# Latent attention: the even block's exponential behind the last step's high part, the odd block's maximum in two parts, the extra turns in the last step

## The reference, cut to what matters

```
def _attend_dense(q, k, v):
    s = einsum('bqhd,bkhd->bhqk', q, k) * (QK_DIM ** -0.5)
    pr = softmax(s, axis=-1)
    return einsum('bhqk,bkhd->bqhd', pr, v)
...
k_all = concatenate([k_lat, k_ctx], axis=1)      # 1024 latent + 256 context keys
v_all = concatenate([v_lat, v_ctx], axis=1)
o = lax.map(lambda qi: _attend_dense(qi, k_all, v_all), qb)   # blocks of 128 queries
...
return (ga * (attn_o @ w_o_attn) + gb * (four_o @ w_fourier)) @ w_out
```

## Time and profile before

| | |
|---|---|
| median of three runs | 2403.45 us |
| the profiled execution's own time | 2400.3 us |
| its span | 2398.5 us |
| PE busy over the span | 94% |
| DVE, ACT busy over the span | 60%, 43% |
| granted TensorE clock, mean | 0.974 |
| attention's units, first maximum to last exponential | 1536 to 1859 us |

### The profile page before, as it was taken

One profiled execution on the slowest core, in us unless ns is written; L12 is line 12 of the kernel. 1 busy time (PEld: TensorE's weight loads), 2 busy tenths in 40 slices (PEclk: granted clock), 3 DMA queues, 4 the chain that ended last, 5 costly groups with the idle time before them and its releaser, 6 DMA issues.

```text
span 2398.5 us, 27813 instructions
## 1 busy us (share of the span) xinstructions
PE 2244.9 (94%) x11294; PEld 1861.8 (78%) x11294; DVE 1434.9 (60%) x2191; ACT 1023.1 (43%) x1586; POOL 273.4 (11%) x362
## 2 busy tenths in 40 slices
PE   5999899999999999999999998898898999499997
PEld 4898787888888888878888787677777775378886
DVE  6667535454554454467422138767667645689997
ACT  4677424122122122144321135466666313378785
POOL 2011001010010011000000015400000100111121
PEclk9999999999999999999999999999999999699998
DMA  3122611232332342232222021000000621989996
GB/s 141 45 71 80 224 49 53 75 119 96 110 129 91 97 145 95 90 116 41 75 88 68 25 73 46 18 1 1 1 1 30 235 75 52 352 317 378 388 387 203
DMA packets 79184, 280.71 MB, mean 117 GB/s; under 512 B 9872, under 2 KB 10000, under 8 KB 77392
## 3 DMA queue, kind: packets, MB, share of 16 engines
q1 hardware_dynamic: 48240, 172.77, 20.0%
q0 software_dynamic: 29664, 101.96, 13.6%
q10 hardware_dynamic: 1152, 4.19, 0.4%
HBM read 243.24 MB, written 35.66 MB: 116 GB/s over the span
## 4 chain that ended last, share of the span: by engine, by line
PE 77%; DVE 13%; ACT 7%; DMA 2%; issue 1%; POOLq 0%; SPq 0%; ACTq 0%; DVEq 0%
PE psum L98 23%; PE psum L99 23%; PE psum L100 23%; DVE small L2603 3%; ACT PB L2537 3%; DVE MP_lo L2640 2%; ACT MP_hi L2567 1%; PE psum L1015 1%; PE psum L2472 1%; PE psum L988 1%; DVE w_lo L232 1%; DMA gal<-gas 1%; PE psum L2483 1%; PE psum L3212 1%; PE psum L2985 1%
## 5 line engine op out<-in xcount | busy, mean ns | idle before, releaser
L98 PE MATMUL psum<-U_hi,w_hi 128*128 128x512 f32 (+1 forms) x1216 | 480.5, 395 | 14.5 <-DVE w_lo L232 9.3
L99 PE MATMUL psum<-U_lo,w_hi 128*128 128x512 f32 (+1 forms) x1216 | 477.9, 393 | 0.0
L100 PE MATMUL psum<-U_hi,w_lo 128*128 128x512 f32 (+1 forms) x1216 | 476.9, 392 | 0.0
L223 ACT ACTIVATE w_hi<-raw 128x1024 fp32r<-128x1024 f32 (+2 forms) x163 | 162.4, 1002 | 305.4 <-PE psum L100 300.8
L98 PEld LDWEIGHTS psum<-U_hi,w_hi 128*128 128x128 f32 (+1 forms) x1216 | 229.3, 189 | 68.7 <-issue 10.7
L100 PEld LDWEIGHTS psum<-U_hi,w_lo 128*128 128x128 f32 (+1 forms) x1216 | 229.3, 189 | 50.5 <-issue 0.8
L99 PEld LDWEIGHTS psum<-U_lo,w_hi 128*128 128x128 f32 (+1 forms) x1216 | 229.6, 189 | 47.4 <-issue 0.5
L232 DVE TENSOR_TENSOR w_lo<-raw,w_hi 128x1024 fp32r<-128x1024 f32 (+2 forms) x163 | 188.8, 1166 | 109.6 <-ACT w_hi L223 109.2
L98 PE MATMUL psum<-a_hi,w_hi 128*128 128x512 f32 x512 | 199.2, 389 | 0.0
L99 PE MATMUL psum<-a_lo,w_hi 128*128 128x512 f32 x512 | 199.2, 389 | 0.0
L100 PE MATMUL psum<-a_hi,w_lo 128*128 128x512 f32 x512 | 199.2, 389 | 0.0
(11 more groups left out here) (407 smaller groups left out, 4689.6 us busy)
## 6 DMA issues: line engine op xcount, KB each, us to landing
rawe<-in_w_e SPq DMA_DIRECT2D x112, 512.0 KB, 15.2
mraw<-in_w_mod POOLq DMA_DIRECT2D x128, 256.0 KB, 2.9
rawx<-in_w_e SPq DMA_DIRECT2D x56, 512.0 KB, 16.3
raw<-in_w_up SPq DMA_DIRECT2D x32, 512.0 KB, 3.6
raw<-in_w_dn SPq DMA_DIRECT2D x32, 512.0 KB, 3.6
raw<-in_w_e SPq DMA_DIRECT2D x24, 512.0 KB, 16.0
X<-in_xT SPq DMA_DIRECT2D x4, 1024.0 KB, 9.4
raw<-in_w_q SPq DMA_DIRECT2D x8, 512.0 KB, 4.4
```

The lines of the kernel that those rows point to most:

```text
L98: e.matmul(o, l[0], r[0], start=first, stop=False, skip_group_check=skip)
L99: e.matmul(o, l[0], r[1], start=False, stop=False, skip_group_check=skip)
L100: return e.matmul(o, l[1], r[0], start=False, stop=last, skip_group_check=skip)
L223: act.e.activation(w_hl[x.place][0][:, 0:x.width], w_raw[x.slot][:, 0:x.width], ACT.Copy).then_inc(w_hi, 1)
```

## The change

Four things change, all in the order of work or in what waits for what; no matmul, no transfer and no tile is added or taken away.

1. The exponential of the even block goes from step t = 3 to t = 4, and so behind the high part of step 4 on ACT. It waits for `part(m + 1, 0)`, not for its own maximum alone.
2. The maximum of the odd block is taken in two parts: columns 0 to 255 (the half bank it shares with the even block) right behind the even block's maximum at t = 2, columns 256 to 1279 at t = 4, and then the smaller of the two negated results (`larger`). The wait of the odd block's maximum for the even block's exponential is gone.
3. The extra turns: `turn_q` part 1 goes from (g, t) = (3, 1) to (3, 4), `turn_k` part 1 from (1, 1) to (1, 4), and parts 0 and 2 of `turn_k` change places, so that the one at (0, 1) is the small one.
4. In the merge, the last iteration no longer prepares the tile behind `T_AO[6] + 4`; its high and low part are made one place later.

```
     nmx = small[:, 0:8]
+    nmp = [small[:, 24 + 2 * i:26 + 2 * i] for i in range(2)]
...
-        x = {(2, 4): ("turn_q", h + 2, 0), (3, 1): ("turn_q", h + 2, 1), (0, 1): ("turn_k", h + 1, 0),
-             (0, 4): ("turn_k", h + 1, 2), (1, 1): ("turn_k", h + 1, 1)}.get((g, t))
+        x = {(2, 4): ("turn_q", h + 2, 0), (3, 4): ("turn_q", h + 2, 1), (0, 1): ("turn_k", h + 1, 2),
+             (0, 4): ("turn_k", h + 1, 0), (1, 4): ("turn_k", h + 1, 1)}.get((g, t))
...
-        m = {0: 2 * u + 3, 3: 2 * u + 4}.get(t, -1)
+        m = {0: 2 * u + 3, 4: 2 * u + 4}.get(t, -1)
...
         def exponential(m):
-            act.wait_ge(*at_s.dve("max", m))
+            act.wait_ge(*(at_s.dve("max", m) if m % 2 else at_s.dve("part", m + 1, 0)))
...
         def largest(m):
             dve.wait_ge(*at_s.pe("logits", m))
-            if m % 2:
-                dve.wait_ge(*at_s.act("exp", m - 1))
             dve.e.tensor_reduce(nmx[:, m % 8:m % 8 + 1], s_of(m), AX.X, ALU.max, negate=True).then_inc(
                 *at_s.dve.one("max", m))
+
+        def part(m, i):
+            dve.wait_ge(*at_s.pe("logits", m - 1 + i))
+            dve.e.tensor_reduce(nmp[m // 2 % 2][:, i:i + 1], s_of(m, *((256, TA) if i else (0, 256))), AX.X, ALU.max,
+                                negate=True).then_inc(*at_s.dve.one("part", m, i))
+
+        def larger(m):
+            dve.wait_ge(*at_s.dve("part", m, 1))
+            p = nmp[m // 2 % 2]
+            dve.e.tensor_tensor(nmx[:, m % 8:m % 8 + 1], p[:, 0:1], p[:, 1:2], ALU.min).then_inc(
+                *at_s.dve.one("max", m))
...
-            if s_chunk(n) and t in (2, 4):
-                largest(2 * u + 4 + t // 4)
+            if s_chunk(n) and t == 2:
+                largest(2 * u + 4)
+                part(2 * u + 5, 0)
+            if s_chunk(n) and t == 4:
+                part(2 * u + 5, 1)
+                larger(2 * u + 5)
...
     def merge_act(act):
         for j in range(8):
-            make_hi(act, T_AO[j] + 4)
+            make_hi(act, T_AO[min(j, 6)] + 4)
...
-                make_lo(dve, T_AO[j] + 4)
+                make_lo(dve, T_AO[min(j, 6)] + 4)
```

More of the change, by code:

```diff
@@ L2401, in _program @@
             at_s.pe.plan(("logits", 2 * u + 4 + t // 4))
-            at_s.dve.plan(("max", 2 * u + 4 + t // 4))
+            at_s.dve.plan(*(("max", 2 * u + 4), ("part", 2 * u + 5, 0)) if t == 2 else
+                          (("part", 2 * u + 5, 1), ("max", 2 * u + 5)))
         if exp_at(n) is not None:
```

## The result

The changed kernel takes 2371.28 us, the median of four runs (2369.89 to 2376.11), against 2403.45 us before (four runs, 2400.88 to 2407.56); the ratio is 0.987 with a 95% interval of 0.985 to 0.989. Forecast were 2375.3 us, range 2366 to 2391.

What follows compares the result with a forecast made beforehand. No engine was full: a chain through DVE and ACT held up PE. Terms by kind of unit summed to -28.1 us, which from 2403.45 gave 2375.3 us, range 2366 to 2391.

Steps and rivals of the forecast that it cites:

- The part maximum, exponential, high part, low part leaves the chain: Unit without extras: low parts 3 and 4 and the long maximum run beside the even exponential; 8.25 us against 9.16.
- The split costs DVE 0.35 us a unit: Odd block's maximum: parts of 0.42 and 1.21 us plus a small operation cost DVE some 0.35 us more a unit.
- rival A: Split maximum: each part costs nearly a whole maximum, a unit loses 0.58 us, time 2393; chance 0.15.
- An extra at t = 4 costs PE 0.44 and a bank wait of 0.37: Units with an extra turn at t = 4: 8.1 + 0.44 + 0.37 = 8.91 us.
- Rival B: Turn behind an extra: still waits 1.43 us, not 0.37, so no gain, time 2402; chance 0.05.
- D: Rival for whole heads: PE loses the added waits, a head nears PE's own 34.4 us, time 2356; chance 0.05.
- g = 3, 9.82: Units at g = 3: the small key extra and step 2's wait for low part 1 give 9.82 us against 10.19.
- g = 1 with rows, 11.5: Units at g = 1 with row extras, heads 2, 4 and 6: 11.5 us against 10.71, three units, +2.3.
- Three units without extras, 0.91 less each: g = 2 and 3 of head 6 and first of head 7: 8.25 us against 9.16, -2.7 together.
- The keys' wait costs 0.7: g = 1: next head's chunk 0 waits for the key turn's low part; +0.70 makes the unit 9.61 us.
- The merge, 0: End of the merge: moving the weight tile's low part changes nothing, at most about 1 us either way.
- rival C: Attention units: short PE waits bring the clock down once in every unit, 31 to 43 us, time 2407; chance 0.05.

Runs made afterwards that it cites:

- e2: Kernel before with only the later even exponential and the split odd maximum, extra turns and merge as before: 2375.62 us, ratio 0.9884.
- e3: Changed kernel with the odd maximum taken whole at t = 4, behind the even exponential: 2399.95 us, ratio 0.9985.
- e4: Changed kernel with the even exponential back at t = 3, the maximum still split: 2404.73 us, ratio 1.0006.
- e8: Changed kernel with one more 256-column reduction on DVE at t = 2, between the even maximum and the odd one's first part: 2374.93 us (one run).
- e5: Changed kernel with the extra turns rotated by one unit, so the last keys are made a unit earlier: 2367.91 us, ratio 0.9854.
- e9: Changed kernel with the merge as before the change: 2372.83 us, ratio 0.9871.
- e10: The changed kernel itself, measured again: 2374.25 us against 2403.82 before, ratio 0.9879.
- e1: Kernel before with only the extra turns in their new places: 2398.65 us, ratio 0.9983.

## Why the prediction was right

The mechanism held, and so did the range and the forecast, though the sum came out so close partly by luck, as the last paragraphs show. All but one of what it named as signs came (g = 3 was 9.45, not 9.8): 8.25 without extras (8.25 measured), 8.91 at g = 0 and 2 (8.78, 8.85), 9.61 at g = 1 (9.66), reductions of 0.42 and 1.21 (0.41, 1.21 to 1.22), PE's idle time down to 13 (12), a wait for `kT_lo` in each of seven heads (0.9).

Step by step:

- *The part maximum, exponential, high part, low part leaves the chain*: shown by e2, e3 and e4. It needs both the split and the move.
- *The split costs DVE 0.35 us a unit*: 0.41 + 1.22 + 0.16 is 0.31 over the 1.48 of before. The slope of two other reductions was right, and e8 shows why it costs nothing: at t = 2 the time is free. So rival A is out by the durations. The Trainium skill, "VectorE: DVE Perf Modes", section "The TRN2 errata — SBUF-src ops pay a fixed extra latency per instruction", has (N + 151)/0.96 ns for a float32 `tensor_tensor` add, not for a reduction. Carried over to the three instructions it gave the estimate of 0.32, and the trace agrees (0.31). The advice that the prediction took from that section, pieces of at least 512 elements, did not decide: the 256-column piece stands where DVE has time to spare (e8).
- *An extra at t = 4 costs PE 0.44 and a bank wait of 0.37*: here 8.78 and 8.85, 0.1 less than forecast. In the g = 0 unit from 1668.67 the chunk starts at 1672.94 and takes 0.70, and the turn behind it starts at 1673.90: a bank wait of 0.26. Rival B, a bank wait of 1.43, didn't come. Neither did D: a common head takes 36.74 us, not PE's own 34.4.
- *g = 3, 9.82*: 9.45 measured, a miss of 0.37 in six units. The term was ACT's: I let each high part hold ACT for 0.61 us, its duration. In the changed kernel, where ACT's work stands back to back, the exponential starts 0.49 after the high part (1810.86 to 1811.35). Two or three such places bring the odd exponential 0.4 earlier, and so the low part that g = 3 waits for. It starts 5.33 after the turn of step 4 where I had 5.80, and the turn of step 2 follows it:

```profile
1660.59 0.60 PE L2474 MATMUL psum<-ident,PB 128*128 128x128 f32 x4
...
1663.98 1.33 ACT L2539 ACTIVATE PB<-psum,small 128x1280 f32<-128x1280 f32 x1
...
1665.92 0.69 DVE L2651 TENSOR_TENSOR MP_lo<-psum,MP_hi 128x512 fp32r<-128x512 f32 x1 [0.85 <-ACT MP_hi L2569]
...
1666.66 0.66 PE L2474 MATMUL psum<-ident,PB 128*128 128x128 f32 x4
```

  Without extras it didn't show, since chunk 0 started 1.46 after the exponential, where I had 1.35 (1811.35 to 1812.81).
- *g = 1 with rows, 11.5*: 10.12, but in heads 2 and 4 the unit behind it is 10.01 and not 8.91. The two together are 20.13 against 20.4: about the right wait, on the other side of the even maximum.
- *Three units without extras, 0.91 less each*: only g = 3 of head 6 was one (9.15 to 8.25). The one ahead of it stands behind the row extras of head 6 and went from 9.26 to 9.41, and the first of head 7 also holds a high part of the output of 1.05 us on ACT (`oT_hi`) and its low part of 1.22 on DVE, and went from 10.44 to 10.09. The three bring 1.1 us, not 2.7.
- *The keys' wait costs 0.7*: shown by e5, 0.8 in common heads.
- *The merge, 0*: shown by e9 for the last tile; what comes behind it varies by more than such an edit could bring.
- *The clock*: rival C is out. One fall of the clock before and one after, the first unit apart. In e10, without it, the units take 285.4 us.

The sum gave -27.2 us for the units (-26.7 without the term of the clock) and -0.9 behind them. The traces gave -27.9, and -29.3 with the falls of the clock taken out of both. Behind the units the last odd exponential starts 5.02 us after the last even maximum, 5.58 before, so 0.6 earlier and not 0.9. The medians gave -32.2 and -29.6 in the two measurements. The last few microseconds are within the scatter of the runs (2400.88 to 2407.56 before), and I can't say more of them.

That the units' sum is so near is in part luck, for large misses cancel. Without the falls of the clock, e10 against before by kind of unit, forecast and then measured: g = 0, -11.9 and -12.4; g = 2, -12.1 and -9.8; g = 3, -2.2 and -4.5; g = 1 without rows, +1.2 and +1.6; g = 1 with rows, +2.3 and -1.8; the three above, -2.7 and -1.1; the start, -1.3 and -1.4. The two lines that touch the row extras miss by 4.1 and 2.3 in opposite directions.

What the prediction didn't see: how little of the gain is edit 3's, some 4 us of 29. It priced it as a part of the whole and never asked what each edit would do alone. When I did ask, for e1 and e4, the sum missed by 10 and 12 us. In e1 that is because it forgot that an extra also pushes the turn of step 0 behind low part 4; in e4 I take it for the same. In the changed order that low part is early, and the omission cost nothing.

## What to carry to other kernels

Where no engine is full, write the loop of a unit as a chain of starts, each with the row that gives its length, check that it gives the period of before (9.16 here), and only then move something. Here the period of the changed order came out to a tenth for the plain unit and for most with one extra; where extras and rows stand together, or a ring of buffers was forgotten, it missed by 0.4 to 1.4 us. Ask for each moved instruction which ring of buffers it takes a place in, since it shifts who waits for whom there, two places on. A resource shared by two stages (the half bank here) can be released by doing its small part early; that is worth nothing by itself if the next thing in the same queue is still late.

## What the runs showed of the hardware that I had not expected

- Behind a high part of 0.59 us on ACT an instruction that needn't wait (the next high part, or the exponential) starts after 0.47 to 0.49 us: 0.1 us before the first has ended. The 1.33 us exponential with its 0.20 us accumulator read holds ACT for 1.30.
- After the first unit the clock fell once in the 284 us in which PE was busy 96% of the time, in a stretch where it was busy 8.70 of 9 us. The two units that it touched took 2.5 us more (0.5 and 2.0) than in e10, where the clock did not fall. So one such fall is more than half of what edit 3 brings beside the others. Waits of PE of 0.9 us, seven of them, brought no fall.
- The exponential ran in the same time beside reductions that read other PSUM banks: the 64 of them take 1.320 to 1.341 us, against 1.322 to 1.332 before.
